# Seven of eight output tiles turned by VectorE in blocks and by transfers, a reordered first norm, and clearings and sums that move

## The reference

```python
xn = rmsnorm(x, norm_mix_g)
gq, gk, gv, gg, ga, mu, mi, mf, mo, rx, ry, gates = split(xn @ w_in + b_in)
o_gla = head_rmsnorm(gla_chunked(q, k, v, log_sigmoid(ga @ w_gla_a2 + b) / 16, S0)) * silu(gg)
o_m   = head_rmsnorm(mlstm_chunked(mq, mk, mv, mi, log_sigmoid(mf), C0, n0, m0)) * sigmoid(mo)
o_r   = rglru(conv(rx), ...) * gelu(ry)
mix   = sum over the branches of sigmoid(gates_b) * (o_b @ w_branch_b)
x     = x + mix @ w_out
u     = rmsnorm(x, norm_ffn_g) @ w_up                    # 1024 -> 5632
ua, ub = split(causal_dwconv(u, width 3, state_ffn_conv))
x     = x + (gelu(ua) * ub) @ w_down                     # 2816 -> 1024
y     = x * rsqrt(mean(x * x, channels) + 1e-6) * norm_f_g
```

## Time and profile before

| what | us |
|---|---|
| median of 3 runs | 974.2 (973.9 to 974.26) |
| the profiled execution | 974.83 |
| its span, first to last instruction | 973.1 |
| PE busy in it | 959.4 (99%) |
| DVE busy | 539.4 (55%) |
| ACT busy | 402.9 (41%) |
| POOL busy | 313.0 (32%) |

### The profile page before, as it was taken

How to read it: one execution, slowest core, us unless ns; L and a number is a source line. 1 busy time by engine, 2 the same in 40 slices (tenths; PEclk the granted TensorE clock), 3 DMA queues, 4 the chain that set the end, 5 groups by cost and what they waited for, 6 DMA issues and landing times.

```text
span 973.1 us, 19320 instructions
## 1 busy us (share of the span) xinstructions
PE 959.4 (99%) x7510; PEld 941.1 (97%) x7510; DVE 539.4 (55%) x906; ACT 402.9 (41%) x584; POOL 313.0 (32%) x301
## 2 busy tenths in 40 slices
PE   9999999999999999999999999999999999999996
PEld 8999999899999999999999999999999999999996
DVE  5396247578645457864227477777777777312122
ACT  6642433377626545223323354444444444212122
POOL 2564423246333224334444621111111110244440
PEclk9999999999999999999999999999999999999999
DMA  5325423234232223534655233333322222522322
GB/s 152 87 67 129 100 66 83 65 80 132 65 100 55 66 66 99 152 95 103 132 110 82 86 89 90 89 91 90 90 87 87 86 86 81 145 81 83 89 60 92
DMA packets 189426, 89.62 MB, mean 92 GB/s; under 512 B 31614, under 2 KB 187908, under 8 KB 189375
## 3 DMA queue, kind: packets, MB, share of 16 engines
q1 hardware_dynamic: 171749, 79.16, 30.7%
q10 hardware_dynamic: 17626, 9.74, 3.8%
HBM read 82.29 MB, written 6.32 MB: 91 GB/s over the span
## 4 chain that ended last, share of the span: by engine, by line
PE 45%; issue 34%; POOL 19%; ACT 1%; DMA 1%; POOLq 0%; DVE 0%; DVEq 0%
PE ps L613 42%; POOL wlo L534 19%; PE ps L1046 1%; PE ps L602 1%; DMA xtok<-x_prompt 1%; PE ps L672 0%; ACT junk L1150 0%; PE ps L638 0%; POOLq L568 0%; PE ps L631 0%; ACT xtok L1166 0%; PE ps L1037 0%; PE ps L1038 0%; ACT whi L1128 0%; POOL blkc L524 0%
## 5 line engine op out<-in xcount | busy, mean ns | idle before, releaser
L534 POOL TENSOR_TENSOR wlo<-stage,whi 128x384 fp32r<-128x384 f32 (+3 forms) x231 | 280.6, 1242 | 407.7 <-ACT whi L1128 317.8
L613 PE MATMUL ps<-xh,whi 128*128 128x272 f32 x1536 | 322.6, 291 | 2.5 <-POOL wlo L534 1.6
L613 PE MATMUL ps<-xh,wlo 128*128 128x272 f32 x1536 | 318.3, 289 | 0.0
L613 PE MATMUL ps<-xl,whi 128*128 128x272 f32 x1536 | 317.4, 288 | 0.0
L613 PEld LDWEIGHTS ps<-xh,whi 128*128 128x128 f32 x1536 | 242.8, 189 | 7.2 <-issue 2.8
L613 PEld LDWEIGHTS ps<-xl,whi 128*128 128x128 f32 x1536 | 242.0, 189 | 0.0
L613 PEld LDWEIGHTS ps<-xh,wlo 128*128 128x128 f32 x1536 | 240.5, 189 | 0.0
L1128 ACT ACTIVATE whi<-stage 128x1024 fp32r<-128x1024 f32 (+3 forms) x59 | 72.1, 1222 | 143.3 <-PE ps L613 129.9
L1137 ACT ACTIVATE whi<-stage 128x1024 fp32r<-128x1024 f32 (+1 forms) x54 | 59.9, 1108 | 144.9 <-PE ps L613 140.5
L586 POOL COPY up<-fst 128x16 f32 (+1 forms) x44 | 25.7, 586 | 227.8 <-DVE ca L2195 227.1
L2195 DVE SCALAR_TENSOR_TENSOR ca<-up,par,ca 128x560 f32<-128x560 f32 x88 | 70.3, 799 | 6.1 <-DVE ca L2195 3.2
(11 more groups left out here) (436 smaller groups left out, 1331.5 us busy)
## 6 DMA issues: line engine op xcount, KB each, us to landing
stage<-w_in SPq DMA_DIRECT2D x52, 512.0 KB, 4.0
stage<-w_up SPq DMA_DIRECT2D x44, 512.0 KB, 3.7
stage<-w_down SPq DMA_DIRECT2D x16, 704.0 KB, 4.5
stage<-w_branch SPq DMA_DIRECT2D x24, 256.0 KB, 4.3
stage<-w_out SPq DMA_DIRECT2D x8, 512.0 KB, 3.7
ch<-state_mlstm_C ACTq DMA_DIRECT2D x4, 512.0 KB, 4.2
s_mlstm_C<-ch ACTq DMA_DIRECT2D x4, 512.0 KB, 4.4
xq<-x_prompt SPq DMA_DIRECT2D x32, 64.0 KB, 3.7
```

The source lines that it names most:

```text
L534: ins = pool.tensor_tensor(wlo[:, slot, a:b, 0:n], stage[:, slot, a:b, 0:n], whi[:, slot, a:b, 0:n].bitcast(F32), ALU.subtract)
L613: ins = mm(dst[:, r, :], w[:, slot, k0 + k, :], x(k)[:, r * HT:(r + 1) * HT], start=first and k == 0 and q == 0, stop=last and k == n - 1 ...
```

## The change

1. Output tiles 0 to 6 are no longer turned by PE. DVE turns `yb` in blocks of 32x32 within each group of 32 partitions into a new buffer `yt` (one instruction of 128x544 per tile), and SP moves the blocks to their place in `ytok` with 20 transfers per tile (16 of 32x4x32 elements, 4 of 32x32; runs of 128 bytes). DVE then multiplies by the gain in place. Ten of the 20 transfers of tile 6 are issued by ACT. SP's loop over tiles becomes straight code: after the two loads of tile m come the transfers of tile m - 2, behind a wait for that tile's turn and for the landing of the transfers before.
2. In the first norm ACT's two scalings move behind all squares and roots.
3. Step `rowc` moves from unit 2 to unit 1, ahead of `a2`.
4. `fraw` is cleared by POOL behind the second w_out tile's `wlo`, and SP's wait for `ssa` becomes a wait for that clearing and for the first turned tile of x.
5. Of the sums over channels, those of `yss` for token tiles 2 to 4 move ahead of the sums of tiles 0 and 1, each in a PSUM bank that stays open.
6. Four small loads count on another semaphore, so that PE's first transposes of parameters wait for them too.

The diff, cut to its core:

```diff
+        yt = at("yt", [P, 2, T], 36864 + 26624)
...
+        def turned_out(eng, m, parts):
+            for a in parts:
+                q = yt[32 * a:32 * a + 32, m % 2, :].rearrange("p (j f) -> p j f", f=32)
+                c0 = m * P + 32 * a
+                for b in range(4):
+                    eng.dma_start(ytok[32 * b:32 * b + 32, 0:4, c0:c0 + 32], q[:, b:16:4, :]).then_inc(s("y_rows"), 16)
+                eng.dma_start(ytok[0:TS, 4, c0:c0 + 32], q[:, 16, :]).then_inc(s("y_rows"), 16)
...
-        plan(1, 0, ("a2", 0))
-        plan(2, 0, ("a2ln", 0), ("rowc", 0))
+        plan(1, 0, ("rowc", 0), ("a2", 0))
+        plan(2, 0, ("a2ln", 0))
...
-            sp.wait_ge(s("ssa"), 1)
+            sp.wait_ge(s("cleared"), 4)
+            sp.wait_ge(s("xt"), 1)
...
-            with sp.Fori(2, KD) as m:
+            def blocks_out(m, parts):
+                sp.wait_ge(s("y_turned"), m + 1)
+                if m:
+                    sp.wait_ge(s("y_rows"), m * 320)
+                turned_out(sp, m, parts)
+            for m in range(2, KD):
                 down_tile(m)
+                blocks_out(m - 2, range(4))
+            blocks_out(KD - 2, range(2))
...
-            lo_units(U_OUT, U_UP + 2)
+            for u in range(U_OUT, U_OUT + 2):
+                lo(u, u % 2, KT_IN)
+            pool.wait_ge(s("gemm"), U_OUT)
+            pool.wait_ge(s("stored"), 4)
+            pool.memset(fraw[:], 0.0).then_inc(s("cleared"), 1)
+            lo_units(U_OUT + 2, U_UP + 2)
             def row_starts(j, r, first):
...
-            def by_token(r, tiles=range(5)):
+            def by_token(tiles):
                 for t in tiles:
                     n = P if t < 4 else TS
-                    ins = tr(pair(2 + r)[0:n, t * P:(t + 1) * P], yb[:, r, t * P:t * P + n], P)
+                    ins = tr(pair(3)[0:n, t * P:(t + 1) * P], yb[:, 1, t * P:t * P + n], P)
                 ins.then_inc(s("y_tr"), 1)
-            def token_sums(b, tiles):
-                for t in tiles:
-                    n = P if t < 4 else TS
-                    mm(bank(b)[0:n, t:t + 1], yss[:, t * P:t * P + n], ones[:, 0:1], start=True, stop=False)
-                    ins = mm(bank(b)[0:n, t:t + 1], ysq[:, t * P:t * P + n], ones[:, 0:1], start=False, stop=True)
-                ins.then_inc(s("ss_mm"), 1)
+            def token_sum(t, last):
+                n = P if t < 4 else TS
+                return mm(bank(SUM_BANK[t])[0:n, t:t + 1], (ysq if last else yss)[:, t * P:t * P + n], ones[:, 0:1],
+                          start=not last, stop=last)
...
-            pe.wait_ge(s("rstd"), 1)
-            pe.wait_ge(s("x2"), 1)
-            by_token(0)
             def down_tile(i, r):
                 pe.wait_ge(s("x2"), i * 2 + (r + 1))
                 down(i * 2 + (r + 2), 0, r)
                 down(i * 2 + (r + 2), 1, r)
-                pe.wait_ge(s("x2"), i * 2 + (r + 2))
-                pe.wait_ge(s("y_gain"), i * 2 + (r + 1))
-                by_token(1 - r)
             with pe.Fori(0, KD // 2 - 2) as i:
                 for r in range(2):
...
-            pe.wait_ge(s("x2"), m)
-            pe.wait_ge(s("y_gain"), m - 1)
-            by_token(0)
             down_half(1, 0, 2)
             pe.wait_ge(s("x2"), m + 1)
-            pe.wait_ge(s("y_gain"), m)
-            by_token(1, range(2))
+            by_token(range(2))
             down_half(1, 2, 3)
             pe.wait_ge(s("yss"), m)
+            for t in range(2, 5):
+                token_sum(t, False)
             pe.wait_ge(s("ysq"), m + 1)
-            pe.wait_ge(s("y_gain"), m + 1)
-            token_sums(4, range(2))
+            for t in range(2):
+                token_sum(t, False)
+                ins = token_sum(t, True)
+            ins.then_inc(s("ss_mm"), 1)
             down_half(1, 5, KT_DOWN - 5).then_inc(s("gemm"), 1)
             pe.wait_ge(s("x2"), m + 2)
             pe.wait_ge(s("y_gain"), m + 2)
-            by_token(1, range(2, 5))
+            by_token(range(2, 5))
             pe.wait_ge(s("ysq"), m + 2)
-            token_sums(0, range(2, 5))
+            for t in range(2, 5):
+                ins = token_sum(t, True)
+            ins.then_inc(s("ss_mm"), 1)
...
-            scaled(0)
-            scaled(1)
             square(2)
             root(2)
             square(4)
             act.wait_ge(s("sum_sq"), 2)
             root(3)
             root(4)
+            scaled(0)
+            scaled(1)
             hi(0)
...
+            act.wait_ge(s("y_turned"), KD - 1)
+            act.wait_ge(s("y_rows"), (KD - 2) * 320)
+            turned_out(act, KD - 2, range(2, 4))
...
-            v.memset(fraw[:], 0.0)
             v.memset(ssa[:], 0.0).then_inc(s("ssa"), 1)
...
-            def gained(m, r, col):
-                dve.wait_ge(s("y_tr"), m + 1)
-                src = pair(2 + r)
-                v.tensor_tensor(ytok[:, 0:4, bass.ds(col, P)], src[:, 0:4 * P].rearrange("p (t c) -> p t c", t=4),
-                                gfb[:, bass.ds(col, P)].unsqueeze(1).broadcast_to([P, 4, P]), ALU.mult)
-                v.tensor_tensor(ytok[0:TS, 4, bass.ds(col, P)], src[0:TS, 4 * P:5 * P], gfb[0:TS, bass.ds(col, P)],
-                                ALU.mult).then_inc(s("y_gain"), 1)
+            def turned(m, r):
+                dve.wait_ge(s("x2"), m + 1)
+                if not isinstance(m, int) or m > 1:
+                    dve.wait_ge(s("y_rows"), m * 320 - 320)
+                v.transpose(yt[:, r, :], yb[:, r, :]).then_inc(s("y_turned"), 1)
+            def gained(m, col):
+                dve.wait_ge(s("y_rows"), m * 320 + 320)
+                y = ytok[:, 0:4, bass.ds(col, P)]
+                v.tensor_tensor(y, y, gfb[:, bass.ds(col, P)].unsqueeze(1).broadcast_to([P, 4, P]), ALU.mult)
+                y = ytok[0:TS, 4, bass.ds(col, P)]
+                v.tensor_tensor(y, y, gfb[0:TS, bass.ds(col, P)], ALU.mult).then_inc(s("y_gain"), 1)
             dve.wait_ge(s("fns"), 2 * NF)
             dve.wait_ge(s("hl"), NF)
             v.memset(yss[:], 0.0).then_inc(s("y_gain"), 1)
             dve.wait_ge(s("y_gain"), 1)
             output(0, 0, U_DOWN + 1)
+            turned(0, 0)
             squares(0, first=True)
             output(1, 1, U_DOWN + 3)
             dve.wait_ge(s("late_in"), 656)
-            gained(0, 0, 0)
+            turned(1, 1)
+            gained(0, 0)
             squares(1)
             def out_step(i, r):
-                dve.wait_ge(s("y_tr"), i * 2 + (r + 1))
                 output(i * 2 + (r + 2), r, i * 4 + (U_DOWN + 2 * r + 5))
-                gained(i * 2 + (r + 1), 1 - r, i * (2 * P) + (r + 1) * P)
+                turned(i * 2 + (r + 2), r)
+                gained(i * 2 + (r + 1), i * (2 * P) + (r + 1) * P)
                 squares(i * 2 + (r + 2))
```

More of the change, by code:

```diff
@@ L60 @@
 GATE_OF = [0, 2, 1]
+SUM_BANK = (4, 4, 0, 1, 5)
 (PB_QKV, PB_MU, PB_RX, PB_RY, PB_GG, PB_MO, PB_GATE) = (0, 8, 12, 16, 20, 24, 28)
@@ L411, in _ @@
             for w, name in enumerate(("state_mlstm_conv", "state_rglru_conv")):
-                sp.dma_start(craw[:, w, :], io[name][0].rearrange("b w c -> (b w) c")).then_inc(s("craw_in"), 16)
-            sp.dma_start(h0raw[:], io["state_rglru_h"][0]).then_inc(s("craw_in"), 16)
-            sp.dma_start(nraw[:], io["state_mlstm_n"][0].rearrange("b h d -> (b h) d")).then_inc(s("craw_in"), 16)
+                sp.dma_start(craw[:, w, :], io[name][0].rearrange("b w c -> (b w) c")).then_inc(s("praw_in"), 16)
+            sp.dma_start(h0raw[:], io["state_rglru_h"][0]).then_inc(s("praw_in"), 16)
+            sp.dma_start(nraw[:], io["state_mlstm_n"][0].rearrange("b h d -> (b h) d")).then_inc(s("praw_in"), 16)
             sp.wait_ge(s("cleared"), 2)
@@ L490, in down_tile @@
                 for r in range(2):
-                    if isinstance(m, int):
+                    if m < 2:
                         free_stage(m * 2 + (U_DOWN + r))
@@ L678, in start @@
                 pe.wait_ge(s("xl"), KD)
-                pe.wait_ge(s("praw_in"), 16 * N_PRAW)
+                pe.wait_ge(s("praw_in"), 16 * N_PRAW + 64)
                 n0, n1, n2 = P_LAM + 4, 2 * 2 * NF, 2 * 2 * NF + 2
@@ L683, in start @@
                 tr(bank(4)[:, P + n1:PAR_N], praw[0:n2, 2, :], n2).then_inc(s("par_tr"), 1)
-                pe.wait_ge(s("craw_in"), 64)
                 for w in range(2):
@@ L1610, in _ @@
             act.wait_ge(s("ss_mm"), 3)
-            func(fstat[:, 2:4], bank(0)[:, 2:4], ACT.Sqrt, bias=eps, scale=1.0 / D_MODEL)
-            func(fstat[0:TS, 4:5], bank(0)[0:TS, 4:5], ACT.Sqrt, bias=eps[0:TS], scale=1.0 / D_MODEL).then_inc(s("std"), 1)
+            func(fstat[:, 2:4], ps[:, 2:2 + 2 * 513:513], ACT.Sqrt, bias=eps, scale=1.0 / D_MODEL)
+            func(fstat[0:TS, 4:5], bank(5)[0:TS, 4:5], ACT.Sqrt, bias=eps[0:TS], scale=1.0 / D_MODEL).then_inc(s("std"), 1)
             out_scaled(3, 2)
@@ L2285, in _ @@
             c7 = slice((KD - 1) * P, KD * P)
-            dve.wait_ge(s("y_tr"), KD - 2)
```

(6 more changed lines are left out.)

## The result

| kernel | median, us (runs) | ratio to before, 95% interval |
|---|---|---|
| before | 974.23 (4) | |
| after | 968.6 (4; 968.2 to 969.0) | 0.9942 [0.9924, 0.9959] |
| after, a second series | 968.09 (5) beside 973.89 (11) | 0.9940 [0.9926, 0.9953] |

The change makes the kernel 5.6 us faster; 5.2 were forecast. The profiled execution of after takes 968.2 us, its span is 966.5 (973.1 before).

A forecast was written before the change was run, and what follows sets the result against it. PE, busy 99% of the span, was taken to bound the kernel. Tiles -3.85, `fraw` -1.1, first norm -0.3, `rowc` +0.1 and sums 0 gave -5.2 us: 974.2 to 969.0 us, range 966.2 to 974.0.

The forecast's parts named there:

- Output tiles: Output tiles 0 to 6: seven groups of five PE transposes at 0.55 us each fall away, 3.85 us less.
- SP's queue: w_down tiles: 20 issues of 0.63 us, 12.6 us, cost nothing; rival, over 0.70 an issue PE waits, chance 0.21.
- my own formula: SP's queue: at p us per issue the last w_down first-load costs PE 100p - 69.5 us; even at p = 0.70.
- The room of 7.5 us: w_down loads: how late SP may issue a tile's first load before ACT waits for it; 4.6 us expected used.
- Ten transfers of tile 6 on ACT: Tile 6: issuing ten of its transfers from ACT saves SP ten issues, some 6 us.
- `fraw`: w_out units: clearing on POOL lets SP load the fifth tile earlier, ending PE's wait; 1.1 us less (0 to 1.12).
- First norm: Start: ACT squares tile 2 earlier, once it has landed at 9.0; 0.3 us less, bounds 0 and 1.3.
- `rowc`: Units 6 to 9: 2.5 us new wait at unit 6, less 0.25, 0.60 and 1.5 of slow clock: 0.1 us more.
- Sums: End: three `yss` sums moved ahead win 0.6 us there, which the matmuls ahead lose; 0, within 0.5 either way.
- The turns do bite: Against the rival that `gprep` runs early without delaying unit 6's `wlo`: 2.1 us less, 966.8 us, chance 0.15.
- The clock doesn't fall behind the longer idle time: Against the rival that the clock falls after the 2.5 us wait at unit 6: 970.5 us, chance 0.17.
- PE is freed: Against the rival that ACT and POOL set the output tile period, losing the 3.85 us: 972.9 us, chance 0.04.

The follow-up runs named there:

- before again: The kernel before, unaltered, run and profiled once more: 973.9 us, ratio 0.9996.
- both attempts to remove it: Changed kernel with `decays` one visit later on ACT, 968.69 us; the same with the last product of `gprep` also put behind `rows`, 967.62 us.
- tile 6 on SP: Changed kernel with all 20 transfers of tile 6 issued by SP, none by ACT: 971.66 us, ratio 0.9974 to before.
- 24 issues: Changed kernel with four of each tile's 20 transfers cut in two, the same bytes: 982.09 us, ratio 1.0085 to before.
- `decays` later: Changed kernel with step `decays` one visit later on ACT, bringing the copy of unit 6 ahead of three exponentials: 968.69 us, ratio 0.9942 to before.

## Why the prediction was right, point by point

- **Output tiles, -3.85.** Right: -3.87 alone, -3.70 with the moved sums.
- **SP's queue, nothing lost.** Right in its outcome, and in part by luck: two errors went against each other. The issue time of 0.63 was right where nothing disturbs it: an issue takes 0.60 us and the next starts 0.64 after it. What I left out is that single issues take far longer. In the tiles of after, the first transfer behind the w_down loads takes 0.6 to 1.6 us, and four others take 1.2 to 1.7 (one is the 937.00 above). So a tile's twenty take 13.1 to 14.7 us, at the tile shown 14.2 or 0.71 each, not 12.6. By my own formula 0.71 is past the even point (100 x 0.71 - 69.5 = 1.5 us lost). It is not lost because the other end was too high: the transfers land in 1.9 us, not 3, and SP's two loads stand between, so that wait is hidden. The room of 7.5 us that I expected to be used to 4.6 was used up to 0.4 at the tile shown, and to 0.1 at the next. Four issues more put it past the edge.
- **Ten transfers of tile 6 on ACT.** I called the saving some 6 us of issue. Without it DVE's product comes 6.2 us later (958.61 for 952.38), but DVE idles 2.30 and 1.12 us between its steps there (in after, before 955.89 and 957.96) and works that off: 2.6 us are left, and 0.9 of slow clock make it 3.6.
- **`fraw`, -1.1.** Right: -1.0 to -1.4 against the four profiles with the old order (314.68 to 315.10), +1.5 when undone. I counted the idle time and not what follows it: behind each wait PE's first pair takes 0.49 to 0.52 in place of 0.41, and the offsets grow by more than the bracket (0.41 for 0.25, 0.83 for 0.60, and the stage's 1.40 for 1.12).
- **First norm, -0.3.** Right over all profiles, and not seen in the pair of the result. With the new order unit 1 starts at 26.42 to 27.45 us in nine profiles, median 26.66; with the old one at 26.90 to 27.05 in four, median 26.96. The mechanism holds: ACT's square of tile 2 now starts when the tile has landed (8.67 to 9.68 us; 9.15 to 9.31 with the old order), and unit 1 starts 17.7 to 17.8 us behind that square in all profiles but one. Where the tile lands late, as in after, nothing is gained.
- **`rowc`, +0.1.** The sum was right by luck: its terms were off and cancel. The wait at unit 6 costs 1.57 in place of 2.5: the copy of unit 6 came 0.5 us earlier, and the turns cost 2.1, not all of the 2.77. Against it stand 0.41 and 0.42 at units 7 and 8 (I had 0.25 for one) and 0.83 behind unit 9 (0.60): 1.57 - 1.66 = -0.1, as 58.16 + 15.16 against 58.20 + 15.22 in the second profile of before. The failed step is the clock: "without that idle time so should the slow stretch: ... 1.5 us" took one fall for a rule. Behind the wait the clock falls in some executions and not in others; where it falls it costs 1.5 us of the stage (16.75 against 15.2), which is why the two first profiles differ by 6.6 us and the medians by 5.6 to 5.8. The Trainium skill, "TensorE: Matmul & The Clock Gate", section "Part 1: The HAM clock gate (the "warmup" mystery)", says that the moment at which the clock rises under matmuls shifts from run to run; here it is the fall that differs from run to run, three in six profiles.
- **Sums, 0.** 136.14 to 136.16 with the move, 135.97 without: it costs 0.2 us, within the 0.5. (The 0.2 for a pair can't be read from the earlier trace rows, which has 0.36 for it.)
- **The rivals.** The turns do bite (2.67 against 4.8). The clock doesn't fall behind the longer idle time. PE is freed. SP's queue was the live one: 0.21 for it was not too much.

The whole: between two profiles in which the clock doesn't fall, before again and after, the stages up to the last sum add up to 964.64 - 959.51 = 5.1 us, close to the 5.2 forecast. The medians differ by 5.6 to 5.8.

How often the clock falls can be counted beyond the profiles, since every run has its mean granted clock on record. The profiles with a fall have 0.996; those without it, and without a long wait at the end, have 0.997 or 0.998. Of 52 such runs of before and its unaltered copy, 17 have 0.996 or less and take 975.2 us on average, 35 have more and take 973.7: again 1.5 us. Over all kernels with the wait behind unit 9, 22 of 72 runs have 0.996 or less, over those without it none of 30 (tile 6 on SP and 24 issues are left aside, since their clock is also low at the end). As far as a mean over the whole run can tell, then, the fall comes only with the wait, in about three runs of ten; taking the wait away saves about 22 / 72 x 1.5 = 0.5 us on average, an estimate that the series are too short to show.

Open: single runs of before go from 973.1 to 976.1 in 45, those of after from 967.4 to 969.0 in nine. `rowc` moved alone, at 0.997 or 0.998 in all eleven runs, still goes from 972.8 to 975.3. What varies there wasn't found.

## What to carry to other kernels

Here work taken off the engine that bounds counted in full, and the trace of before gave it within 0.02 us (3.85 for 3.87). The risk is in the queue that takes the work over: work out how full that queue will be per period, issue by issue, with the slow ones behind loads in it, and not with the undisturbed issue alone. A wait that another engine's order makes (here `wlo` against DVE's instructions) moved in both attempts to remove it: count what arrives next before you pay for it. A stretch of slow clock seen in one profile is one draw: take a second profile, and look at the mean granted clock of every run, before it enters a sum.

## What the runs showed that was not expected

- An issue takes 0.60 us on SP, whether the transfer has 128 runs of 128 bytes, 64 or 32 (medians of 0.602, 0.597 and 0.599), and the next one starts 0.64 us after it. In these three sizes the time goes by the number of transfers and not by the bytes, so cutting a transfer in two doubles it.
- Some issues take far longer, at two kinds of places. One is right behind a w_down load: 0.6 to 1.6 us in after, 2.2 in the kernel with 24 issues. The other has no w_down load in flight (857, 872, 922 and 937 us in after): each time one transfer of 16 KB of the kind `instruction` (queue q8 of the page) starts within 0.4 us of the slow issue's start. In the kernel with 24 issues SP's issue at 961.40 and ACT's at 961.72 are both slow (1.84 and 1.53) beside such a transfer at 961.5. That the two coincide is what the traces show; the cause isn't.
- Three `wlo` instructions take 2.67 us beside DVE's clearings or its instructions on four columns, and 4.8 to 5.0 beside `gprep` or `rows`. The Trainium skill, "SBUF — State Buffer", section "SBUF: two separate sides", has the two engines lock a shared port for a whole instruction; these rows agree, and so do two of DVE's instructions on four columns beside that `wlo` of 2.67 us (`decays` later), at 0.93 and 0.95 in place of 0.17.
- 1408 columns cleared on POOL took 1.28 us, 0.9 ns a column; 256 took 0.30.
